# Modulation vectors of a two-layer diffusion backbone: products with 32 stationary columns in four column groups of the array

## The reference

```python
def _modulation(cvec, w, b, n):
    return jnp.split(jax.nn.silu(cvec) @ w + b, n, axis=-1)
...
    for l in range(DEPTH):
        sh1, sc1, g1, sh2, sc2, g2 = [t[:, None, :] for t in _modulation(c, mod_w[l], mod_b[l], 6)]
        csh1, csc1, cg1, csh2, csc2, cg2 = _modulation(c_ctx, mod_w[l], mod_b[l], 6)
        h = _rmsnorm(x, norm1_w[l]) * (1.0 + sc1) + sh1
        y, yc = _token_mixer(h, hc, ...)       # mLSTM, window attention, retention, then w_out
        x = x + g1 * y
        h2 = _rmsnorm(x, norm2_w[l]) * (1.0 + sc2) + sh2
        x = x + g2 * _conv_ffn(h2, ...)
```

## Time and profile before

| what | value |
|---|---|
| median of 3 runs | 3336.56 us (3333.86 to 3338.16) |
| span of the profiled execution, first to last instruction | 3326.9 us |
| TensorE busy in that span | 3099.7 us (93%) |
| VectorE, ScalarE, GpSimd busy | 1220.7, 956.9, 1129.1 us |
| mean granted TensorE clock | 0.968 of 2.4 GHz |
| products of the modulation, busy | 190.0 us |

### The profile page before, as it was taken

The page is one execution under the profiler, slowest core; times in us unless marked ns, Lnnn a source line. Parts: engine busy times, 40 slices in busy tenths (PEclk is TensorE's granted clock), DMA queues, the critical chain, the costliest instruction groups (busy, mean ns, idle before and its releaser), DMA issues. The chain is left out here.

```text
span 3326.9 us, 47831 instructions
## 1 busy us (share of the span) xinstructions
PE 3099.7 (93%) x19520; PEld 2660.7 (80%) x19520; DVE 1220.7 (37%) x2792; ACT 956.9 (29%) x1600; POOL 1129.1 (34%) x614
## 2 busy tenths in 40 slices
PE   6899999999999999999999779899999999989996
PEld 3788887898888997888888657787898778968885
DVE  2344415523333023333333534433532231154455
ACT  2222224432223112222222232222542222233332
POOL 2122240053333433333333232332143335345453
PEclk8999999999999999999999879999999999989998
DMA  5011120012221115211111211111022222222222
GB/s 192 26 52 52 46 88 26 7 53 91 80 83 67 64 58 186 75 64 64 71 64 57 99 55 52 70 58 70 20 80 89 89 89 91 101 95 98 98 89 95
DMA packets 39671, 249.80 MB, mean 75 GB/s; under 512 B 4512, under 2 KB 4896, under 8 KB 14112
## 3 DMA queue, kind: packets, MB, share of 16 engines
q1 hardware_dynamic: 36576, 236.25, 19.8%
q10 hardware_dynamic: 2880, 10.49, 0.8%
HBM read 236.23 MB, written 10.49 MB: 74 GB/s over the span
## 5 line engine op out<-in xcount | busy, mean ns | idle before, releaser
L1868 POOL TENSOR_TENSOR w_rest<-raw,w_head 128x2048 fp32r<-128x2048 f32 (+2 forms) x172 | 740.7, 4307 | 1099.0 <-ACT w_head L1042 1067.0
L687 PE MATMUL psum_products<-w_head,h_head 128*128 128x256 f32 x2368 | 691.4, 292 | 0.0
L687 PE MATMUL psum_products<-w_rest,h_head 128*128 128x256 f32 x2368 | 678.6, 287 | 0.0
L687 PE MATMUL psum_products<-w_head,h_rest 128*128 128x256 f32 x2368 | 677.9, 286 | 0.0
L687 PE MATMUL psum_products<-h_head,w_head 128*128 128x512 f32 (+3 forms) x1696 | 599.8, 354 | 19.4 <-POOL h_rest L1894 17.1
L687 PE MATMUL psum_products<-h_head,w_rest 128*128 128x512 f32 (+3 forms) x1696 | 598.1, 353 | 0.0
L687 PE MATMUL psum_products<-h_rest,w_head 128*128 128x512 f32 (+3 forms) x1696 | 596.9, 352 | 0.0
L687 PEld LDWEIGHTS psum_products<-w_head,h_head 128*128 128x128 f32 x2368 | 462.9, 195 | 2.6 <-issue 1.2
L687 PEld LDWEIGHTS psum_products<-w_rest,h_head 128*128 128x128 f32 x2368 | 463.5, 196 | 0.5
L687 PEld LDWEIGHTS psum_products<-w_head,h_rest 128*128 128x128 f32 x2368 | 462.8, 195 | 0.0
L1042 ACT ACTIVATE w_head<-raw 128x2048 fp32r<-128x2048 f32 (+2 forms) x172 | 307.6, 1789 | 472.7 <-PE psum_products L687 427.9
(11 more groups left out here) (236 smaller groups left out, 4135.9 us busy)
## 6 DMA issues: line engine op xcount, KB each, us to landing
raw<-in_stream SPq DMA_DIRECT2D x198, 1024.0 KB, 4.7
raw<-in_stream SPq DMA_DIRECT2D x20, 512.0 KB, 3.3
residual<-stage ACTq DMA_DIRECT2D x16, 512.0 KB, 2.7
stage<-residual SPq DMA_DIRECT2D x14, 512.0 KB, 4.7
stage<-in_x SPq DMA_DIRECT2D x8, 512.0 KB, 5.9
stage<-in_ctx SPq DMA_DIRECT2D x4, 512.0 KB, 8.2
out<-stage ACTq DMA_DIRECT2D x4, 512.0 KB, 2.6
rope_r<-in_rope_r SPq DMA_DIRECT2D x2, 768.0 KB, 4.2
```

The costliest lines, as they stand in the source:

```text
L687: return nc.tensor.matmul(o, a, b, start=start, stop=stop)
L1868: G.tensor_tensor(wl[:, s["sp"] % 2, 0:n], raw[:, s["n"] % 2, 0:n], wh[:, s["sp"] % 2, 0:n].bitcast(F32), ALU.subtract).then_inc(*ev.mark( ...
```

## The change

The two vectors are padded with zeros to 32 stationary columns (`c_silu`). The eight products of a slice are now one piece, and product k writes partitions 32 (k % 4) to 32 (k % 4) + 31 of the bank, that is, it uses the 32 columns of the array with that number: k tiles 0 and 4 add up in group 0, and so on. VectorE copies all 128 partitions, and the turning product sums the four groups, by a constant `pick` of 128 x 2 in place of the unit matrix. `vrow` has two buffers, with a wait for the turn two slices before. A slice is two steps (products, turn) where it was five, the turn of a slice stands behind the next slice, and the counts of steps that `ticks` spreads are changed with it.

```diff
@@ make_plan
         for l, n in islice(modulation, count):
             s = cols("mod_w", l, n * COLS, splits=False)
-            for piece in range(4):
-                yield step("vector", s, l=l, n=n, piece=piece)
-                if piece == 0 and turn:
-                    yield step("vector", **turn)
-            turn = dict(slot=s, l=l, n=n, piece=4)
+            yield step("vector", s, l=l, n=n, piece=0)
+            if turn:
+                yield step("vector", **turn)
+            turn = dict(slot=s, l=l, n=n, piece=1)
         yield step("vector", **turn)
...
-            pieces = 4 * len(pairs(ctx)) + 1
+            pieces = 4 * len(pairs(ctx)) - 2
             fill = chain(vectors(1), fill)
             ticks("mtiles", len(tiles) + 5, fill, pieces, l=l, hd=hd, tiles=tiles)
...
             fill = vectors(3)
-            ticks("rstates", 4, fill, 4, l=l, hd=hd)
-            ticks("rtiles", len(tiles) + 4, fill, 11, l=l, hd=hd, tiles=tiles)
+            ticks("rstates", 4, fill, 2, l=l, hd=hd)
+            ticks("rtiles", len(tiles) + 4, fill, 4, l=l, hd=hd, tiles=tiles)
...
-        ticks("norms", len(tiles) + 2, fill, 5 * 2 * D // COLS, l=l, use="mid", tiles=tiles, gen=gen)
+        ticks("norms", len(tiles) + 2, fill, 2 * 2 * D // COLS, l=l, use="mid", tiles=tiles, gen=gen)
@@ TensorE
-                    if piece < 4:
-
-                        for k in (2 * piece, 2 * piece + 1):
-                            last = mm(bank[0:2, 0:COLS], cvec[:, 2, k, :], w[:, k, :], k == 0, k == KD - 1)
+                    if piece == 0:
+                        for k in range(KD):
+                            q = 32 * (k % 4)
+                            last = mm(bank[q:q + 32, 0:COLS], csilu[:, k, :], w[:, k, :], k < 4, k >= 4)
...
-                            last = mm(bank[:, 2 * ct:2 * ct + 2], vrow[0:2, ct * P:(ct + 1) * P],
-                                      c("ident")[0:2, 0:2])
+                            last = mm(bank[:, 2 * ct:2 * ct + 2], vrow[:, st["n"] % 2, ct * P:(ct + 1) * P], c("pick"))
                         last.then_inc(*ev.mark("pe", "bank", st["bank"]))
+                        ev.now[("vturn", l, st["n"])] = {"pe": ev.count["pe"]}
@@ VectorE
+            V.memset(csilu[:], 0.0).then_inc(*ev.mark("dve", "c0"))
...
-            V.tensor_scalar(cvec[:, 2], cvec[:, 1], 0.5, None, ALU.mult).then_inc(*ev.mark("dve", "silu_c"))
+            V.tensor_scalar(csilu[:, :, 0:2], cvec[:, 1], 0.5, None, ALU.mult).then_inc(*ev.mark("dve", "silu_c"))
...
-                if kind == "vector" and st["piece"] == 3:
+                if kind == "vector" and st["piece"] == 0:
                     dve.wait_ge(*ev.at("vrow", l, st["n"]))
-                    V.tensor_copy(vrow[0:2, :], psg[0:2, st["bank"] % RING, 0:COLS]).then_inc(
+                    if (l, st["n"]) >= (0, 2):
+                        dve.wait_ge(*ev.at("vturn", *((l, st["n"] - 2) if st["n"] >= 2 else (l - 1, st["n"] + 22))))
+                    V.tensor_copy(vrow[:, st["n"] % 2, :], psg[:, st["bank"] % RING, 0:COLS]).then_inc(
                         *ev.mark("dve", "vrow_sb", l, st["n"]))
```

More of the change, by code:

```diff
@@ L45 @@
 URING = 6
-ARENA_BYTES = 74 * 1024
+ARENA_BYTES = 74 * 1024 - 32
 EPS = 1e-6
@@ L78, in constants @@
         col_f=127 - r[:, :1], col_b=r[:, :1], rot=rot, flip=np.eye(P)[::-1],
-        neg_half=np.full((P, 1), -0.5), one=np.ones((P, 1)), cd=np.full((P, 1), float(P)))
+        neg_half=np.full((P, 1), -0.5), cd=np.full((P, 1), float(P)),
+        pick=(r % 32 == j)[:, :2])
     place, cols = {}, []
@@ L425, in backbone @@
         par = sb("par", [P, DEPTH, NPAR])
-        cvec = sb("cvec", [P, 3, KD, 2])
-        vrow = sb("vrow", [P, COLS])
+        cvec = sb("cvec", [P, 2, KD, 2])
+        csilu = sb("c_silu", [P, KD, 32])
+        vrow = sb("vrow", [P, 2, COLS])
         vec = sb("vec", [P, DEPTH, 6 * KD, 2])
@@ L1014, in _ @@
                 if s is not None:
-                    if kind == "vector" and st["piece"] == 4:
+                    if kind == "vector" and st["piece"] == 1:
                         continue
@@ L1097, in _ @@
                     act.wait_ge(*ev.last("act"))
-                    nc.scalar.activation(gm[:, 1, :], gm[:, 3, :], ACT.Ln, bias=c("one")).then_inc(
+                    nc.scalar.activation(gm[:, 1, :], gm[:, 3, :], ACT.Ln, bias=c("ones")[:, 0:1]).then_inc(
                         *ev.mark("act", "lnf", l))
@@ L1234, in _ @@
                         act.wait_ge(*ev.last("act"))
-                        nc.scalar.activation(x, x, ACT.Ln, bias=c("one")).then_inc(*ev.mark("act", "rabs", l))
+                        nc.scalar.activation(x, x, ACT.Ln, bias=c("ones")[:, 0:1]).then_inc(*ev.mark("act", "rabs", l))
                     for ct in (0, 1):
```

## The result

Timed beside each other, the changed kernel takes 3284.24 us (median of 4 runs, 3283.09 to 3285.47) and the kernel before 3335.21 us (4 runs, 3331.09 to 3338.16). The ratio is 0.9854, with a 95% interval of 0.9842 to 0.9866: 51 us faster, where 40 had been forecast. The profiled executions stand nearer to each other, 3326.9 and 3283.7 us of span, 43.2 apart, because the execution of the kernel before that was profiled is faster than its four timed runs.

A forecast was written before the change was run, and what follows sets the result against it. Modulation pieces on TensorE's path in retention, VectorE in the mLSTM, loads at the start and DMA in the norm were taken as bounds. Start 9, norm 6.4, mLSTM 6.8, retention 8 and 9.6 sum to 40 us: 3297 us, range 3248 to 3320.

The forecast's parts named there:

- The price of a slice: TensorE's modulation products: records start in order, only different groups overlap, so a slice costs 2.05 us; chance 0.50.
- the rival of full overlap: Modulation slices: a product's two records do not hold up the next group; slice 1.0 us, kernel 3259 us; chance 0.23.
- Retention: Retention heads: layer 0 from 30.45 to 28.5 us, layer 1 from 28.1 to 25.7; 8 and 9.6 us less.
- mLSTM: mLSTM heads: shorter way to layer 0's first numerator, VectorE's copy off layer 1's path; 4.8 and 2 us less.
- I cost the move at nothing: mLSTM heads: GpSimd's split moves earlier, but its 4.5 us VectorE stall is there already; no cost.
- The rival's 36 us: mLSTM: moved split costs VectorE or GpSimd 4.5 us a second time in eight heads; 3333 us; chance 0.07.
- Start: Kernel start: slices every 3.4 us in place of 4.53, first turned tiles at 37.0 us; 9 us less.
- The low clock: Kernel start: if TensorE's clock fell in gaps, a slice would cost up to twice as much, the gain be 4.
- Norm: Norm before the MLP: ticks costed by DMA bytes, plus a shorter end; 38.8 becomes 32.3 us, 6.4 less.
- The arena: Memory: the smaller arena was costed at nothing.
- The sum: Whole kernel: 40 us less, giving 3297 us; each us of a slice counts about 39 us.
- the last three: Outcomes outside the range: groups taking turns 0.15 (3352 us), moved split 0.07 (3333 us), the rest above 3320, 0.05.

The follow-up runs named there:

- group_pairs: Changed kernel with product k in group k // 2 in place of k % 4, so successive products share a group; 3284.17 us.
- one_group: Changed kernel with all eight products of a slice adding up in the first group of 32 columns; 3381.08 us.
- late_split: Changed kernel with the steps in the last stretch of each mLSTM head 4 ticks later, GpSimd's split behind the last deviation; 3275.56 us.
- arena_64: Changed kernel with 64 unused bytes a partition ahead of the arena; 3269.9 us.
- warm: Changed kernel with useless 128-column products where TensorE waits in retention heads, eight a head; 3278.24 us.
- half_twice: Changed kernel with the first four products of each slice issued twice, the first time for nothing; 3295.69 us.

## Why the prediction held, and which of its steps did not

**The price of a slice** failed: "Group 0 must end its first record before its second, and the first record of group 1 stands behind that second one", 2.05 us. The trace has 1.07, group_pairs shows that the order of issue does not bind other groups, and one_group prices no overlap at 3.64. The rival's 1.0 us was right, so that the rival of full overlap had the mechanism. The Trainium skill ("TensorE: Matmul & The Clock Gate", Part 3) gives about 4 ns between starts of packed products and a gain of 2.38 times for three groups; here starts are 7 ns apart and four groups gain 3.64 / 1.07 = 3.4 times, in fp32 with two records. The same part of the Trainium skill says that products keep the order of issue, with no reordering. Taken for records, that would have given my 2.05 us; the runs do not show it: group_pairs has 1.09.

**Retention** held when the slice is put right. 28.5 - 3 x 0.98 = 25.6 for layer 0, measured 25.2; 25.7 - 2.9 = 22.8 for layer 1, measured 22.5. The waits forecast as 1.0 behind the turned keys and 0.75 before the first score are 0.96 and 0.77. What fails is that the next stage starts at full pace: the heads alone give 43 us, and from the first head to the products with `y_head` only 34.7 arrive.

**mLSTM.** Start to first numerator is 5.17 us; the forecast of 6.4 with the slice put right is 5.4. No head has two long VectorE operations, as forecast; the second of layer 0 has none. "I cost the move at nothing" held in the sum: with the slice put right the forecast is 8.7 us for layer 0 and 5.9 for layer 1, and 6.8 and 7.0 came. What was missed is that a better place was to be had, about 2 us a head in layer 0 by late_split, part of it through the clock. The rival's 36 us did not come.

**Start.** Forecast 3.4 us a slice and 37.0 for the first turned tiles; measured (34.70 - 18.17) / 5 = 3.31 and 38.30. This is right by luck: at the lower clock a slice takes 1.94, near my 2.05. At 1.07 the period would be (4.8 + 1.07) / 2 = 2.9 by the same sum, an estimate. The low clock was named in the prediction as a danger and given no share in the sum.

**Norm.** Forecast 32.3, measured 36.2. Loads of `raw` lie in the queue with the loads of tiles and land 6.2 to 10.3 us after issue, so that slices wait 3.9 and 3.6 us for them. The clock falls at the end of each of these waits and of the 4.3 us before the first turned tile, to 0.76 in the mean, and makes most slices 1.94 and turned tiles 1.97, where a slice takes 1.07 and a turned tile 1.09 at the higher clock. I had counted bytes, and nothing for loads that come in a lump behind a wait.

**The arena**, which with its smaller size "I cost at nothing", failed by 11 us by the distance of starts and by 14 by arena_64, through the place of the arena and not its size; the 3 us between the two are open.

**The sum.** With the slice at 1.07 the terms give 40 + 0.98 x 39 = 78 us, and 75 less the 3 that the loads hold back, as the rival of full overlap had it. 43 (51 in the timed medians) came, so 32 are missing in the profiled executions. The ledger says where: the start gave 7.8 of the 12 that full overlap promised, the norm 2.5 of 7.4 (6.4 and one slice, an estimate), the heads 56.9 of 55.7, and the stretches that the change does not touch took 24 back. Of these 24 the distance of starts of the products with y and u accounts for 11, and what is lost between the end of the retention heads and the products with `y_head` for 43.1 - 34.7 = 8.4, of which warm brings back 6.0; about 5 are open. The 8.7 us of late_split are not among them: they come out of a place of the split for which the kernel before paid too. Half of TensorE's busy time at the lower clock, which is what the higher clock would save, is 57 us before and 102 after, with the time before the first entry in both: the clock takes 44 us more of TensorE's time than before, part of it where TensorE would wait anyway. So the forecast of 3297 us lies 13 us from the result by two errors that nearly cancel, a slice too dear and everything around it too cheap; that the number came near is luck. The low stretches of the start and of the norm were not tried by an experiment aimed at them. And the prediction put "0.2 or a bit more" outside its range, where its own chances for the last three add up to 0.27.

## What to carry to other kernels

Where TensorE's busy time falls without its waits going too, look at the granted clock behind each new wait before the saving is counted: eight useless products a head, in waits of about a microsecond, gained 6 us here. When a change adds or resizes a buffer, compare the distance of starts of products that it does not touch; 64 unused bytes were worth 14 us. And the place of a filler step can decide whether a long GpSimd operation lies beside VectorE's last work of a stage: moving it was worth 2 us a head in layer 0 here.

## What was unexpected of the hardware

- Products of fp32 in four groups of 32 columns overlap fully: 16 records in four rounds of 0.2 us, and it makes no difference whether two products in a row use the same group (1.07 and 1.09 us).
- The pace of a full product moves by 2 to 6 ns of 115 to 233 with the address of its operands: 115.3, 118.7 and 120.0 ns for w with y at three places of the arena.
- Fed with packed products of 1.94 us every 3.3 us, TensorE keeps the pace of 1.2 GHz through the whole start, 38 us; the kernel before left it at 10.5 us, with its records of two columns following each other without a break from 6.3 us on, and half_twice, with 24 records a slice, was at the higher pace from 9.4 to 12.8 and from 29.9 to 43.5 us.
